# When a two-block transformer kernel loads and applies the second layer's modulation: one chunk moved into the second half of an FFN product, sixteen units moved three weight units later

## The reference

```python
cond = jax.nn.silu(c)
for l in range(DEPTH):                                    # DEPTH = 2
    mod = (cond @ ada_w[l] + ada_b[l])[:, None, :]        # 6 * 1024 numbers
    sh1, sc1, g1, sh2, sc2, g2 = jnp.split(mod, 6, axis=-1)
    h = rmsnorm(x, norm1_g[l]) * (1 + sc1) + sh1
    x = x + g1 * hybrid_mixer(h, cos, sin, w_in[l], b_in[l], rel_bias[l], w_branch[l], w_out[l])
    h = rmsnorm(x, norm2_g[l]) * (1 + sc2) + sh2
    x = x + g2 * swiglu(h, w_ffn_in[l], w_ffn_out[l])
return rmsnorm(x, final_g)
```

## Time and profile before

| | us |
|---|---|
| three runs | 1458.05, 1460.41, 1464.55 |
| the profiled execution, its own time | 1457.7 |
| its span, first to last instruction | 1455.9 |
| PE matmul busy / weight loads busy | 1434.6 / 1202.6 |
| POOL, ACT, DVE busy | 1211.2, 756.6, 723.7 |
| second FFN output half on PE | 430.81 to 459.38 |
| projection chunks of layer 1 on PE | about 461.4 to 544.51 |

### The profile page before, as it was taken

The page is one execution under the profiler, slowest core; times in us unless marked ns, Lnnn a source line. Parts: engine busy times, 40 slices in busy tenths (PEclk is TensorE's granted clock), DMA queues, the critical chain, the costliest instruction groups (busy, mean ns, idle before and its releaser), DMA issues.

```text
span 1455.9 us, 21556 instructions
## 1 busy us (share of the span) xinstructions
PE 1434.6 (99%) x7600; PEld 1202.6 (83%) x7600; DVE 723.7 (50%) x1556; ACT 756.6 (52%) x1275; POOL 1211.2 (83%) x986
## 2 busy tenths in 40 slices
PE   7999999999999999999999999999999999999997
PEld 5898777799988987778888888778888888788886
DVE  7863654766643754745566304454650044655202
ACT  4435675644445345765544445674654346665442
POOL 3799989898878987559898997966999977789995
PEclk9999999999999999999999999999999999999999
DMA  9994556689875986337676565644556655445561
GB/s 362 397 357 160 187 171 229 227 306 316 315 266 162 399 310 214 114 99 231 221 243 201 187 204 171 188 142 145 188 188 202 217 163 184 130 162 201 194 197 58
DMA packets 149559, 313.35 MB, mean 215 GB/s; under 512 B 10934, under 2 KB 31818, under 8 KB 149451
## 3 DMA queue, kind: packets, MB, share of 16 engines
q1 hardware_dynamic: 147696, 310.62, 63.0%
q10 hardware_dynamic: 1756, 1.35, 0.3%
HBM read 310.87 MB, written 1.06 MB: 214 GB/s over the span
## 4 chain that ended last, share of the span: by engine, by line
PE 93%; DVE 3%; ACT 1%; POOL 1%; issue 1%; DMA 1%; SPq 0%; POOLq 0%; DVEq 0%; ACTq 0%
PE bank L804 58%; PE bank L849 12%; PE bank L850 8%; PE bank L847 5%; PE bank L1012 1%; PE bank L996 1%; POOL lo_units L741 1%; PE bank L885 1%; PE bank L982 1%; DMA x_rows<-in_x 1%; PE bank L1095 1%; PE bank L1064 1%; PE bank L1028 1%; PE bank L1111 1%; PE bank L1054 0%
## 5 line engine op out<-in xcount | busy, mean ns | idle before, releaser
L741 POOL TENSOR_TENSOR lo_units<-raw_units,hi_units 128x512 fp32r<-128x512 f32 (+3 forms) x928 | 1151.0, 1276 | 223.7 <-ACT hi_units L1390 222.7
L1390 ACT ACTIVATE hi_units<-raw_units 128x1024 fp32r<-128x1024 f32 (+1 forms) x470 | 482.8, 1031 | 410.5 <-PE bank L804 248.6
L804 PE MATMUL bank<-hi_units,turned 128*128 128x512 f32 (+3 forms) x1600 | 441.7, 391 | 2.1 <-DVE turned L1928 1.7
L804 PEld LDWEIGHTS bank<-hi_units,turned 128*128 128x128 f32 x1600 | 291.9, 189 | 53.7 <-issue 3.3
L850 PE MATMUL bank<-turned,lo_units 128*128 128x256 f32 x1024 | 288.4, 282 | 0.0
L804 PE MATMUL bank<-hi_units,turned_wide 128*128 128x512 f32 x992 | 274.6, 391 | 0.0
L849 PE MATMUL bank<-turned,hi_units 128*128 128x512 f32 x736 | 260.1, 398 | 0.0
L804 PE MATMUL bank<-lo_units,turned 128*128 128x512 f32 (+3 forms) x800 | 253.5, 384 | 0.8 <-POOL lo_units L741 0.5
L804 PEld LDWEIGHTS bank<-hi_units,turned_wide 128*128 128x128 f32 x992 | 185.3, 188 | 38.5 <-issue 0.5
L850 PEld LDWEIGHTS bank<-turned,lo_units 128*128 128x128 f32 x1024 | 194.5, 190 | 0.2
L804 PEld LDWEIGHTS bank<-lo_units,turned 128*128 128x128 f32 x800 | 150.2, 189 | 30.8 <-POOL lo_units L741 3.7
(11 more groups left out here) (266 smaller groups left out, 1294.3 us busy)
## 6 DMA issues: line engine op xcount, KB each, us to landing
ada_units<-in_ada_w SPq DMA_DIRECT2D x88, 512.0 KB, 7.4
raw_units<-in_w_ffn_tiles SPq DMA_DIRECT2D x72, 512.0 KB, 5.2
raw_units<-in_mlp_w_out SPq DMA_DIRECT2D x64, 512.0 KB, 3.3
raw_units<-in_mlp_w_tiles SPq DMA_DIRECT2D x56, 512.0 KB, 3.3
raw_units<-in_w_in SPq DMA_DIRECT2D x56, 458.0 KB, 9.7
raw_units<-in_w_in SPq DMA_DIRECT2D x48, 512.0 KB, 6.9
raw_units<-in_w_ffn_out SPq DMA_DIRECT2D x44, 512.0 KB, 4.0
raw_units<-in_moba_w_qkv SPq DMA_DIRECT2D x24, 512.0 KB, 3.7
```

Of the source, the lines that this page charges most:

```text
L741: pool.tensor_tensor(LO[:, s, b, 0:w], RAW[:, u["slot"], b, 0:w], HI_[:, s, b, 0:w].bitcast(F32), ALU.subtract).then_inc(lo_ready.sem, lo_ ...
L804: ins = pe.matmul(BANK[2 * c["pair"] + t][:, 0:w], (A[a] if A is BT else A[:, a])[:, part, t * P:(t + 1) * P], W[:, s, b, 0:w], start=(i = ...
L1390: act.activation(HI_[:, s, 0:n, 0:w], RAW[:, u["slot"], 0:n, 0:w], ACT.Copy)\
```

## The change

Four edits. In the first FFN's stage, the modulation chunk (1, 5) is taken out of the spread list and `tail` goes from 3 to 9; this leaves the places of all other units of that stage as they were. The four units of (1, 5) stand now between the units of the second output half, after units 132, 134, 136 and 138. Its sum on PE and its drain on DVE are moved behind the first projection chunk of layer 1 (`carried`), and DVE processes its units between draining the first output half and the second. In the projection stage of layer 1, `lead` goes from 6 to 9: the 16 units of chunks (1, 6) to (1, 9) begin three weight units later and stand closer together; with them, chunks (1, 6) and (1, 8) are summed and drained one projection chunk later than before.

```diff
-    def phase(parts, adas, summed=True, lead=0, tail=0):
+    def phase(parts, adas, summed=True, lead=0, tail=0, carried=()):
...
+            if vec_args == parts[0][0] and args == parts[0][1]:
+                chunks.extend(carried)
             if summed:
                 chunks.extend(done)
...
-            phase(parts, [(l, c) for c in (6, 7, 8, 9)], lead=6)
+            phase(parts, [(l, c) for c in (6, 7, 8, 9)], lead=9, carried=[gate1])
...
-            phase(parts, [(l, 10), (l, 11)] + [(l + 1, c) for c in range(6)], lead=SPLIT, tail=3)
+            phase(parts, [(l, 10), (l, 11)] + [(l + 1, c) for c in range(5)], lead=SPLIT, tail=9)
         else:
             phase(parts, [(l, 10), (l, 11)], lead=SPLIT, tail=8)
-        for cc in range(1 if l + 1 < DEPTH else 0, D // CW):
+        if l + 1 < DEPTH:
+            rest = chunk(("ffo", l, 1), ("w_ffn_out", l), 0, FFN // P, CW, CW)
+            gate1 = ada(l + 1, 5)
+            for n, u in enumerate(rest["units"]):
+                stream.append(u)
+                if n % 2 and n // 2 < len(gate1["units"]):
+                    if n // 2 == len(gate1["units"]) - 1:
+                        stream.extend(ada_vecs(l + 1, 5))
+                    stream.append(gate1["units"][n // 2])
+            continue
+        for cc in range(D // CW):
             put(chunk(("ffo", l, cc), ("w_ffn_out", l), 0, FFN // P, cc * CW, CW))
...
-                ada_upto(pos_in_stream[min(nxt["units"][-1]["index"] + 1, len(pos_in_stream) - 1)])
+                first_half = key == ("ffo", 0, 0)
+                ada_upto(pos_in_stream[min(nxt["units"][0 if first_half else -1]["index"] + 1, len(pos_in_stream) - 1)])
...
             add_to_x(("ffo", l, 0), 5 * D, 1.0, following, D if more else None)
+            if more:
+                ada_upto(1 + max(n for n, u in ada_units if (u["l"], u["c"]) == (1, 5)))
             across_rms(("ffo", l, 1), 5 * D, 1.0, following, D if more else None, 0,
```

## The result

The changed kernel takes 1462.58 us (median of 20 runs, 1460.33 to 1468.68), the kernel before 1458.11 beside it (20 runs, 1454.95 to 1464.55). The ratio is 1.0035, 95% interval 1.0025 to 1.0045: 5.1 us slower (3.6 to 6.6), less than the half per cent (7.3 us) that the prediction counts as no difference. The forecast was 5.2 us slower.

The account below looks back on a forecast made before the run. PE, busy for 99% of the span, was taken as the bound. Terms 0 + 0 + 5.2 = 5.2 us slower gave 1462.9 on the profiled 1457.7, about 1465.5 as median; forecast's range 1463 to 1468, with other cases 1458.5 to 1471.

Parts of the forecast that it names:

- Part 1: Chunk (1, 5) moved into the second output half: work moved, not added, and worth 0 in the profiled execution.
- the cover of 4.2 us: At SP's new wait at (1, 5, 3): unit 139 ready at 446.6, PE wants it at 450.8; costed at 0.
- "it costs nothing": The queue's 12 us standstill before the change, 392.90 to 404.96, costs PE nothing; unit 127 has 2.4 us of cover.
- Part 2, b_in: With lead 9, the eighth projection chunk's b_in starts at 537.7 instead of 530.27, 7.4 us later.
- Unit 173: Eighth projection chunk: rounded from 544.05, PE's last two matmuls on it end near 547.9 instead of 544.51: 3.4 us.
- Unit 178 and the first heads: ACT rounds unit 178 from 551.7, 7.1 us later; PE's first heads start at 553.3, 5.2 us late.
- Nothing gives it back: Behind the first heads every engine waits in order and the stages are PE's, so the 5.2 us stay lost.
- The hidden case: b_in starts by about 532.5 or the burst lands faster, covers hold: -1 to +2 us on 1460.4; chance 0.27.
- The gain elsewhere: In usual runs PE may wait at units 126 to 128 behind the standstill; removed, time 1454 to 1459; chance 0.08.
- The clearly slower case: SP's wait at (1, 5, 3) overdraws its cover, PE losing 4 us more in the second half: 1469.5 or more; chance 0.15.
- The estimate from the Trainium skill: By the page's transfer fit, unit 178 lands 10.2 us after the vector, a loss of some 1.3 us; not used.

Follow-up runs that it names:

- The sixth experiment: The changed kernel with 12 added PE matmuls, results unread, while it stands for unit 173: +4.4 us (+2.6 to +6.1) on the kernel before.
- the ninth: The changed kernel with vector b_in(1, 7) put behind weight unit 173 instead of ahead of it: +8.0 us (+5.1 to +10.9) on the kernel before.
- part 1 alone: The changed kernel with lead 6 instead of 9, chunk (1, 5) still moved; timed twice: +1.9 us and -1.3 us on the kernel before.
- the third experiment: The changed kernel with vectors b_in(1, 7) and b_gate(1, 0) put behind weight unit 178: -0.1 us (-1.5 to +1.2) on the kernel before.
- 10: The changed kernel, DVE adding the seventh projection chunk and draining (1, 8) before units (1, 9, 2) and (1, 9, 3): +5.2 us on the kernel before.
- 2: The kernel before with lead 9 instead of 6, chunk (1, 5) not moved: +4.2 us (+2.6 to +5.8) on the kernel before.
- 5: The changed kernel with lead 7 instead of 9: +5.0 us (+3.2 to +6.7) on the kernel before.
- 8: The changed kernel with SP holding unit (1, 5, 3) until PE has used unit 137: +13.7 us (+10.9 to +16.3) on the kernel before.
- 4: The kernel before with SP holding b_in(1, 7) until the seventh projection chunk is added up: +6.3 us (+4.4 to +8.2) on the kernel before.
- 7: The changed kernel with SP holding b_in(1, 7) until PE has used unit 172: +10.1 us (+8.0 to +12.2) on the kernel before.
- twelfth: The kernel of the ninth with 16 added PE matmuls before the first heads, results unread: +6.4 us (+3.4 to +9.3) on the kernel before.

## Why the prediction was right

**The number.** 5.2 us were forecast and 5.1 (3.6 to 6.6) measured. That close an agreement is luck in part: the traces put the loss at 4.8, and two terms below were off by more than the difference. The time itself was given as 1465.5, with 1463 to 1468 as the forecast's own range, and is 1462.58. It stood on the median of three runs, 1460.41, where twenty give 1458.11.

**Part 1.** Costed at 0, and right within what can be measured: -1.3 and +1.9 us in two sessions, 0.0 in both traces. SP stood at (1, 5, 3) until 442.61 - 4.70 = 437.91, where 437.9 was predicted, with no wait of PE. But the cover of 4.2 us was worked out wrongly. It is 2.7, because the last unit behind the wait has less than the first. The rival that rested on it was nearer than the prediction had it. The same look at the first unit alone stands behind "it costs nothing" for the old standstill, where unit 127 had 2.4 us of cover: true in the profiled execution, and 0.7 to 1.1 us short at the last low halves in two others.

**Part 2, b_in.** Predicted at 537.7; it came at 542.47 - 4.70 = 537.77. The two vectors ahead fit as well: 519.71 - 4.70 = 515.0 and 530.88 - 4.70 = 526.2, against 515.0 and 525.8.

**Unit 173.** Rounding was predicted from 544.05 and came at 543.5, its end on PE was predicted at 547.9 and came at 553.85 - 4.70 = 549.15. The term of 3.4 us for this unit was 1.2 too small. Its working had no clock in it: it took full speed behind a gap, as everywhere else in the stretch. Of the second gap, before L1012, only 0.4 us is left in after for this reason. The sixth experiment shows that the error cost nothing here and the ninth that it could have.

**Unit 178 and the first heads.** Predicted at 551.7 and 553.3, measured 551.3 and 552.9. The loss is 4.8 by the trace where 5.2 was the sum; the spacing from the vector to unit 178 was 13.5 us, not 14.0. The claim that the 3.4 of unit 173 lie inside this wait, since both hang on one burst, is shown by the sixth and ninth experiments: without the one gap the other is there. In the eight traces in which the vector stands ahead of unit 173 and is late, the heads follow b_in by 15.1 to 15.8 us.

**Nothing gives it back.** Right: 906.4 us behind the first heads, as in part 1 alone, to the 1 us or so by which the traces differ there.

**The rivals.** The hidden case fell with b_in at 537.8: 7.5 us late against a cover that the eight traces with the vector ahead of unit 173 put at 2.1 to 2.8. The gain elsewhere didn't appear in a time: no version with the earlier transfers is measurably faster than before, the third experiment included. Its mechanism does exist, a wait behind the standstill, but in the traces it is 0 to 1.1 us and not more than 5.2. The clearly slower case did not occur, and begins with another 2.7 us at (1, 5, 3).

The estimate from the Trainium skill, "DMA: Bandwidth & Descriptors", section Anatomy of one DMA, was a loss of 1.3 us. From the vector to unit 178's rounding it was 13.5 us here, where the estimate from the page's fit is 10.2. That section gives its fit for one transfer issued by GpSimd. Here SyncE issues eight in a row, so the measurement speaks against carrying the fit over to such a burst, and not against the fit.

## What to carry to other kernels

When a change moves a drain, an add or a sum past another, look at what else waits for that event: here it was a ring of small bias vectors, and the wait stood in an in-order queue ahead of megabytes of weights. The vector itself had time; putting it behind the units that are urgent made the same wait free. And read the cover of a wait at every unit queued behind it, not at the first alone: where the maker of units is slower than their user for a while, the last one decides.

## What was unexpected of the hardware

TensorE's clock fell to its lower level (0.50, 1.2 GHz) at some short gaps and not at others, and the length of the gap alone does not sort them. The gaps in the table are PE's idle times before unit 173, but for the ninth experiment (before the first heads) and the last row. Behind a gap unit 173 takes 3.2 us at full clock.

| experiment | gap, us | granted clock behind it | unit 173, us |
|---|---|---|---|
| 10 | 1.81 | 1.00 | 3.2 |
| 2 | 1.92 | 0.61 on the mean | 4.5 |
| 5 | 2.04 | 1.00 | 3.2 |
| 8 | 2.45 | 1.00 | 3.2 |
| the change | 2.59 | 1.00 for 1.3 us, then 0.50 for 3.41 | 4.6 |
| 9 | 3.73 | 0.50 | |
| 4 | 4.42 | 0.50 | 4.9 |
| 7 | 7.04 | 0.50 | 4.7 |
| 8, before unit 139 | 4.91 | 0.50 | |

In the sixth and twelfth, where PE worked through the gap, it stayed at 1.00. The Trainium skill, "TensorE: Matmul & The Clock Gate", section What's actually happening, says that an idle array is gated to 1.2 GHz and gets full speed again only after it has been busy. The traces agree in that every fall here followed a gap and 1.00 came back while PE worked. They also show two things to allow for: gaps of up to 2.45 us without a fall, and a fall that came only after PE was at work again. The loss is 1.3 to 2.6 us each time, and it only counts where no later wait takes it up.
